# Banded attention on one core: the order of values, the row of maxima and the last scores within a head

## What is computed

```python
s = jnp.einsum('bqhd,bkhd->bhqk', qb, kb).astype(jnp.float32) * scale + bias[None]
valid = (start + j - pad) >= 0
s = jnp.where(valid[None, None, None, :], s, MASK_VALUE)
p = jax.nn.softmax(s, axis=-1)
return jnp.einsum('bhqk,bkhd->bqhd', p.astype(vb.dtype), vb)
```

## Time and profile before

| | us |
|---|---|
| median of 3 runs | 1870.58 (1869.71 to 1871.69) |
| the profiled execution, its own time | 1869.13 |
| its span, first to last instruction | 1867.4 |
| TensorE busy | 1755.8 (94%) |
| VectorE busy | 934.6 (50%) |
| ScalarE busy | 726.4 (39%) |
| GpSimd busy | 494.3 (26%) |
| mean granted TensorE clock | 0.985 |

### The profile page before, as it was taken

One profiled execution on the slowest core, in us unless ns is written; L12 is line 12 of the kernel. 1 busy time (PEld: TensorE's weight loads), 2 busy tenths in 40 slices (PEclk: granted clock), 3 DMA queues, 4 the chain that ended last, 5 costly groups with the idle time before them and its releaser, 6 DMA issues.

```text
span 1867.4 us, 35922 instructions
## 1 busy us (share of the span) xinstructions
PE 1755.8 (94%) x14176; PEld 1103.6 (59%) x14176; DVE 934.6 (50%) x2175; ACT 726.4 (39%) x1438; POOL 494.3 (26%) x580
## 2 busy tenths in 40 slices
PE   7799999999999799999999999999999999999986
PEld 5344444444445556666676666766767667666654
DVE  6555554465441236455364553635536355463544
ACT  6322231232110226354362543625436254462643
POOL 1111110111002014143151432514325152241523
PEclk9899999999999899999999999999999999999988
DMA  9435235334515212122211212122122221122101
GB/s 314 143 113 192 91 125 189 131 116 157 169 66 180 76 36 75 49 64 81 59 50 57 64 64 60 66 57 64 52 65 72 58 64 52 58 79 57 64 29 58
DMA packets 142396, 168.87 MB, mean 90 GB/s; under 512 B 7304, under 2 KB 117400, under 8 KB 140200
## 3 DMA queue, kind: packets, MB, share of 16 engines
q1 hardware_dynamic: 141208, 165.50, 27.4%
q0 software_dynamic: 1040, 1.31, 0.4%
HBM read 92.55 MB, written 54.05 MB: 79 GB/s over the span
## 4 chain that ended last, share of the span: by engine, by line
PE 79%; DVE 8%; SPq 4%; DMA 3%; ACT 3%; issue 2%; POOL 0%; POOLq 0%; ACTq 0%
PE bank L859 17%; PE bank L854 16%; PE bank L265 9%; PE bank L245 5%; PE bank L246 5%; PE bank L247 5%; PE bank L880 4%; PE bank L905 4%; PE bank L935 3%; SPq L1358 3%; DVE res L1237 2%; PE bank L960 2%; PE bank L962 2%; DMA kl<-nat 2%; PE bank L961 2%
## 5 line engine op out<-in xcount | busy, mean ns | idle before, releaser
L1311 POOL TENSOR_TENSOR p_l<-p,p_h 128x256 f16<-128x256 f32 (+1 forms) x376 | 383.6, 1023 | 834.0 <-ACT p_h L1087 833.8
L854 PE MATMUL bank<-hT,wa_h 128*128 128x256 f16 x2048 | 351.2, 273 | 1.2 <-DMA hT<-h_split 0.9
L859 PE MATMUL bank<-wa_h,hT 128*128 128x512 f16 x1024 | 319.3, 379 | 0.0
L854 PE MATMUL bank<-hT,wa_l 128*128 128x256 f16 x1024 | 280.0, 273 | 0.0
L1082 ACT ACTIVATE p<-bank 128x256 f32<-128x256 f32 (+1 forms) x376 | 190.2, 506 | 148.8 <-DVE bank L1205 145.2
L1188 DVE CUSTOM_DVE_ANT_0 junk<-bank,bias_q 128x640 bf16<-128x640 f32 (+4 forms) x256 | 199.4, 779 | 53.3 <-PE bank L905 53.3
L854 PEld LDWEIGHTS bank<-hT,wa_h 128*128 128x128 f16 x2048 | 198.2, 98 | 32.1 <-DMA hT<-h_split 1.1
L1087 ACT ACTIVATE p_h<-p 128x256 f16<-128x256 f32 (+1 forms) x376 | 204.4, 544 | 11.9
L245 PE MATMUL bank<-hT,wp_h 128*128 128x512 f16 x512 | 195.6, 382 | 1.5 <-DVE hT L451 1.5
L246 PE MATMUL bank<-hT,wp_h 128*128 128x512 f16 x512 | 195.6, 382 | 0.0
L247 PE MATMUL bank<-hT,wp_l 128*128 128x512 f16 x512 | 195.4, 382 | 0.0
(11 more groups left out here) (109 smaller groups left out, 2934.1 us busy)
## 6 DMA issues: line engine op xcount, KB each, us to landing
xin<-in_x SPq DMA_DIRECT2D x32, 512.0 KB, 5.1
xres<-in_x SPq DMA_DIRECT2D x32, 512.0 KB, 3.4
h_split<-hT SPq DMA_DIRECT2D x16, 1024.0 KB, 6.9
residual<-xres SPq DMA_DIRECT2D x32, 512.0 KB, 2.6
hT<-h_split SPq DMA_DIRECT2D x16, 1024.0 KB, 5.1
res<-residual SPq DMA_DIRECT2D x32, 512.0 KB, 4.0
out<-res SPq DMA_DIRECT2D x32, 512.0 KB, 2.7
wst<-in_w_in SPq DMA_DIRECT2D x16, 512.0 KB, 6.8
```

The lines of the kernel that those rows point to most:

```text
L854: mm = nc.tensor.matmul(bank[:, 0:AT], w, hT2[:, 1 if p == 1 else 0, kt, :], start=(m == 0), stop=(m == 23))
L859: mm = nc.tensor.matmul(bank[:, :].rearrange("p (c n) -> p c n", c=4), hT2[:, 1 if p == 2 else 0, kt, i * P:(i + 1) * P], w, start=(m == 0 ...
L1311: nc.gpsimd.tensor_tensor(p_l[:, h % 2, c + a:c + b], p32[:, s, a:b], p_h[:, h % 2, c + a:c + b], ALU.subtract).then_inc(A["pl_done"], 1)
```

## The change

Within a head, on TensorE, `values` of the head before and `max_rows` of the next head are issued in front of the head's last group of scores. Before, the order was last scores, `max_rows`, `values`; after it is `values`, `max_rows`, last scores. No other engine's order is touched, and no instruction or wait is added or dropped.

```diff
                         if fillers:
                             part(*fillers.pop(0))
-                    scores(t, h, last)
+                    if h > 0:
+                        values(t, h - 1)
                     if h + 1 < HEADS:
                         max_rows(t, h + 1)
-                    if h > 0:
-                        values(t, h - 1)
+                    scores(t, h, last)
```

## The result

| | before | after |
|---|---|---|
| median of the runs, us | 1870.95 (4 runs) | 1896.61 (4 runs, 1895.09 to 1899.06) |
| the profiled execution's span, us | 1867.4 | 1894.0 |
| mean granted TensorE clock | 0.985 | 0.988 |

The changed kernel is slower: ratio 1.0137, 95% interval 1.0124 to 1.0149, +25.7 us. The forecast was 1897.6 us, in a range of 1888 to 1904.

A forecast was written before the change was run, and what follows sets the result against it. TensorE, busy 94% of the span, was taken as the bound. Tiles 2 to 14 +28.3, tile 1 +1.7, tile 0 +0.3, tile 15 -3.3 gave +27.0 us, so 1897.6 us; range 1888 to 1904.

The forecast's parts named there:

- The round trip and its cover: TensorE, row to next head's first scores over ScalarE's copy: 0.83 us, covered by 0.33 us, so 0.50 us new pause.
- Head by head: Tiles 2 to 14, losses: heads 2, 3, 4, 6 0.49 us each, head 1 0.15, head 5 0.39, heads 0 and 7 none.
- The give-back of 0.16 us: Heads after 2 and 3: VectorE about 0.16 us less late against TensorE, twice a tile, 0.32 us back.
- What VectorE gives back: Behind `finish`, `attend` no longer waits for values but for the last scores' bias: 0.32 us back a tile.
- The bound of 1885 us: Whole of the two 0.65 us waits for a maximum absorbs the delay: 1.20 us a tile, +14.3 us.
- the absorbing rival: VectorE's waits in two heads a tile absorb more of the delay if `attend` kept its time: 1885 us, chance 0.07.
- Tile 15: Last tile: values in front fill the row's wait for VectorE, up to 1.15 us; 3.3 us gained in sum.
- The small terms: Tiles 1 and 0, with fewer matmuls of values: 1.7 us and 0.3 us lost.
- sign of being wrong: ScalarE: prediction wrong if a head's first exponential starts later against its scores; put at 0, 8 us if 78 turns lost 0.1.
- The case of the Trainium skill: TensorE clock falls through short pauses between matmul groups on cycling PSUM banks; one head a tile at 1.2 GHz: 1964, chance 0.05.
- the faster rival: Values in front cover TensorE's wait for minus_max; wins only if the round trip were hidden: 1863, chance 0.02.

The follow-up runs named there:

- The row first: Order row of maxima, values, last scores, in place of last scores, row, values in the kernel before: 1888.0 us, ratio 1.0092.
- the row last: Order values, last scores, row of maxima, in place of last scores, row, values in the kernel before: 1906.07 us, ratio 1.0182.
- The longer path: One more ScalarE copy of the row, into a spare buffer, ahead of the copy into qm: 1922.75 us on the new order, 1884.06 us on the old.
- the two experiments on it: `attend` ahead of the last bias, new order: 1888.2 us; `finish` moved from heads 2, 3 to 6, 7 except tile 15: old order 1847.29, new 1878.22 us.
- the old order with `finish` late: Kernel before the change with VectorE's `finish` moved from heads 2 and 3 to 6 and 7, tile 15 as it was: 1847.29 us, ratio 0.9864.

## Why the prediction was right

**The round trip and its cover.** 0.83 us from row to scores in 107 of 128 turns, 0.90 us of values, 1.73 us a turn: as forecast. The exceptions are longer: 1.13 us out of head 0, where ScalarE turns a unit of q in front of the copy, as forecast too, and a few in tile 0 and one in tile 15. The row first (+16.8 us), values first (+25.7) and the row last (+34.8) order the three by what stands behind the row, and each came within about 2 us of its working. For the row first the 16.8 us are no round trip, which is covered there (1.25 us from row to scores), but waits for VectorE, and in tile 15 a lower clock besides. The longer path costs the new order nearly twice what it costs the old.

**Head by head.** From the first scores of one head to those of the next, tile 8: out of head 1 +0.15 us (forecast 0.15), head 2 +0.50 (0.49), heads 3 and 4 +0.32 and +0.33 (0.33), head 5 +0.38 (0.39), head 6 +0.50 (0.49), heads 0 and 7 together within 0.04. Tiles 2 to 14: +28.29 us, forecast 28.3. The give-back of 0.16 us shows one head behind the `finish` that causes it. The row's wait for minus_max is gone in head 1, and the wait for a maximum behind `finish` fell from 0.65 to 0.5 us, as forecast.

**What VectorE gives back.** The mechanism was right and the two experiments on it agree. But I took the waits of 0.65 us as the whole of what was there. They cost 0.82 us each, since the record of the matmul ahead (0.27 us, where the next could start after 0.11) covers the beginning of the wait. The bound of 1885 us for the absorbing rival was wrong for another reason too: it let both waits go in full, but only 0.49 us of new pause lie ahead of each of the two. The run with `attend` in front of the bias gives that rival its condition. It absorbed 0.44 and 0.49 us a tile, and its time was 1888.2 us. That is at the edge of the range and not outside it, where the prediction had put this case. The measured 1896.6 us lies 8 us above it, and the rows of `attend` show why.

**Tile 15.** Forecast -3.3 us, measured -3.9. That they agree is luck in part, for the total hides two things of opposite sign that the sum didn't have. Its heads, from the first scores of head 1 to those of head 7, took 35.13 us and take 30.03, a gain of 5.1. Busy times of that stretch, before:

```profile
1803.15:1838.28 35.13, 25.04 (x300) 18.32 (x301) 22.26 (x65) 23.45 (x47) 20.43 (x23) 0.77 0.17 61
```

and after:

```profile
1833.66:1863.69 30.03, 20.62 (x301) 14.79 (x302) 23.06 (x66) 22.91 (x46) 20.77 (x23) 0.94 0.20 72
```

The granted clock (the column before the last two) is 0.94 for 0.77: besides the filled waits, matmuls ran at full clock that had run at half. I had put the clock only into the range. Against that, one turn failed. Out of head 2, from the start of the block that comes first to the next first scores, 2.16 us were forecast; it took 2.78 (1841.10 to 1843.88), more than the 2.37 of before. From first scores to first scores the head is still 0.51 us shorter (4.88 for 5.39). TensorE first, then ScalarE:

```profile
1841.10 0.19 PE L960 MATMUL bank<-v_h,p_h 128*128 128x65 f16 x1
...
1842.40 0.28 PE L918 MATMUL bank<-ident,m 128*128 128x128 f16 x2 [0.22 <-DVE m L1196]
1842.52 0.27 PE L935 MATMUL bank<-qs,ks 128*128 128x256 f16 x1
1842.63 0.27 PE L937 MATMUL bank<-qm,kl 65*128 65x256 f16 x1
1843.88 0.22 PE L935 MATMUL bank<-qs,ks 128*128 128x128 f16 x1 [0.98 <-ACT qm L1072]
```
```profile
1842.71 0.63 ACT L1087 ACTIVATE p_h<-p 128x512 f16<-128x512 f32 x1
1843.36 0.37 ACT L1072 ACTIVATE qm<-bank 1x256 f16<-1x256 f32 x1
```

ScalarE was still at the fp16 half of the second group's exponential when the row was ready. The end after the heads was 1.2 us longer. In it the 48 matmuls of the last output took 12.66 us at a granted clock of 0.83, for 11.28 at 0.93. In the other ten profiled kernels they took 11.19 to 12.62, and the old order with `finish` late took 12.52 (at 0.84). So it goes with the clock; whether the order has a part in it stays open.

**The small terms.** What lies ahead of tile 2 came out at +2.2 us, forecast 2.0, and that is luck: 1.0 of it lies before tile 0's heads, where the change does nothing and where the twelve profiled executions differ by up to 3.5 us. Tiles 0 and 1 together cost 1.2. Tile 1 cost 1.7 as forecast, tile 0 gained 0.5 where 0.3 of loss was forecast, by its turn out of head 0, which took 6.6 to 7.4 us in the twelve traces. The prediction named as a sign of being wrong that a head's first exponential starts later against its scores. In tiles 2 to 14 it did so in head 2, 1.95 us for 1.68; in no other head, and TensorE lost nothing by it, since the turn cost its 0.49 us.

**The rivals.** The clock stayed at 1.00 in the middle tiles. The heads of tile 7 after the change, the stretch of the earlier trace rows, and then tiles 2 to 14 as a whole:

```profile
1184.07:1229.64 45.57, 41.39 (x487) 31.04 (x485) 30.12 (x84) 31.26 (x63) 24.80 (x26) 1.00 0.14 48
780.00:1828.00 1048.00, 989.78 (x9665) 680.70 (x9664) 526.54 (x1404) 474.92 (x962) 346.25 (x364) 1.00 0.19 59
```

The pauses shown are 4.18 us of 45.57, 9%, at full clock; 4.9 us of 45.6 were forecast. The case of the Trainium skill (TensorE: Matmul & The Clock Gate, "A second HAM failure mode: psum-queue depth-cycling"), where short pauses made the clock swing, did not come about. That VectorE absorbs more is excluded by `attend`'s rows. The mechanism of the faster rival is real, but only the last tile has the waits for it: -4.2 us when the order is changed there alone.

## What to carry to other kernels

When blocks of an in-order engine are swapped, look for a step that goes out to another engine and comes back, measure its round trip where nothing covers it, and count what is left behind it. Here 0.90 us of work that moved from behind the row to in front of it turned 1.23 us into 0.90 + 0.83. Work that can be cut can stand on both sides of such a step: half the values in front hide a wait ahead of the row, half behind hide the one after it, here for a gain of 0.3%. The price of a wait on a pipelined engine is read from start to start against the same place without it, not from the idle time shown.

## What I had not expected

The idle time in front of a matmul was 0.17 us less than its cost: 0.65 us shown and 0.82 us by the starts. In the pause that the change makes it was 0.34 us shown, with 0.50 us of distance more than the old order has.

Moving VectorE's `finish` by four heads, whose waits in the middle tiles are shown as 0.65 us each, was worth 24 us (1.3%), about as much as the reordering lost.
